# Causal mask of the diagonal score block: VectorE addition in PSUM instead of two bf16 products of TensorE per unit

## The reference, cut to what matters

```python
scale = HEAD_DIM ** -0.5                       # HEAD_DIM = 64
sc = jnp.einsum('bqhgd,bhqkd->bhgqk', qb, kg, preferred_element_type=f32) * scale
p = masked_softmax(sc, m_sel)                  # key_pos <= query position
...
diff = tq[:, None] - kpos[None, :]
m_win = (kpos[None, :] >= 0) & (diff >= 0) & (diff < WINDOW)
p = masked_softmax(sc, m_win)
...
def masked_softmax(s, mask):
    s = jnp.where(mask, s.astype(jnp.float32), NEG)      # NEG = -1e30
    return jax.nn.softmax(s, axis=-1) * mask
```

## Time and profile before

| | |
|---|---|
| median of 3 runs | 1780.42 us (1780.27 to 1780.75) |
| the profiled execution | 1778.62 us, its span 1776.8 us, mean clock granted to TensorE 0.997 of full speed |
| TensorE busy (matmuls / weight loads) | 1730.8 us (97%) / 1406.8 us (79%) |
| VectorE busy | 940.1 us (53%) |
| ScalarE busy | 651.3 us (37%) |
| GpSimd busy | 125.3 us (7%) |
| DMA | 174.86 MB, mean 98 GB/s |

### The profile page before, as it was taken

The page is one execution under the profiler, slowest core; times in us unless marked ns, Lnnn a source line. Parts: engine busy times, 40 slices in busy tenths (PEclk is TensorE's granted clock), DMA queues, the critical chain, the costliest instruction groups (busy, mean ns, idle before and its releaser), DMA issues.

```text
span 1776.8 us, 26563 instructions
## 1 busy us (share of the span) xinstructions
PE 1730.8 (97%) x10044; PEld 1406.8 (79%) x10044; DVE 940.1 (53%) x1522; ACT 651.3 (37%) x1152; POOL 125.3 (7%) x252
## 2 busy tenths in 40 slices
PE   7989999999999999999999999999999999999998
PEld 6767777788888888888887777777888888888886
DVE  5688777554454444422357977775453544444223
ACT  4334565522242232221353355654222522223213
POOL 4710000000000000000037000000000000000000
PEclk9999999999999999999999999999999999999999
DMA  7532111122523222222263421111333222222222
GB/s 258 165 97 76 57 56 48 53 103 95 168 72 106 95 94 94 94 95 95 89 246 109 102 80 54 54 49 59 107 107 125 77 95 98 101 96 94 95 95 83
DMA packets 65917, 174.86 MB, mean 98 GB/s; under 512 B 14256, under 2 KB 26576, under 8 KB 65056
## 3 DMA queue, kind: packets, MB, share of 16 engines
q1 hardware_dynamic: 40192, 140.53, 23.6%
q10 hardware_dynamic: 21888, 13.64, 3.1%
q0 software_dynamic: 3744, 19.41, 3.1%
HBM read 162.27 MB, written 7.08 MB: 95 GB/s over the span
## 4 chain that ended last, share of the span: by engine, by line
PE 88%; DVE 6%; DVEq 2%; ACT 2%; issue 1%; DMA 0%; ACTq 0%
PE ps L523 19%; PE ps L525 18%; PE ps L524 18%; PE ps L563 6%; PE ps L561 6%; PE ps L562 6%; PE ps L840 2%; PE ps L827 2%; PE ps L813 2%; DVE ta L1363 1%; PE ps L664 1%; PE ps L552 1%; PE ps L541 1%; DVE wlo L1357 1%; PE ps L816 1%
## 5 line engine op out<-in xcount | busy, mean ns | idle before, releaser
L523 PE MATMUL ps<-xh,whi 128*128 128x512 f32 x1312 | 520.2, 396 | 5.3 <-ACT gates L1173 2.1
L525 PE MATMUL ps<-xh,wlo 128*128 128x512 f32 x1312 | 512.2, 390 | 0.0
L524 PE MATMUL ps<-xl,whi 128*128 128x512 f32 x1312 | 511.5, 390 | 0.0
L1357 DVE TENSOR_TENSOR wlo<-raw,whi 128x1024 fp32r<-128x1024 f32 x264 | 324.7, 1230 | 342.0 <-ACT whi L961 331.7
L961 ACT ACTIVATE whi<-raw 128x1024 fp32r<-128x1024 f32 x264 | 278.6, 1055 | 350.7 <-PE ps L563 234.2
L523 PEld LDWEIGHTS ps<-xh,whi 128*128 128x128 f32 x1312 | 246.9, 188 | 59.5 <-DVE wlo L1357 3.6
L525 PEld LDWEIGHTS ps<-xh,wlo 128*128 128x128 f32 x1312 | 246.6, 188 | 52.7
L524 PEld LDWEIGHTS ps<-xl,whi 128*128 128x128 f32 x1312 | 247.1, 188 | 49.0
L561 PE MATMUL ps<-whi,hh 128*128 128x512 f32 x352 | 137.5, 391 | 0.0
L563 PE MATMUL ps<-whi,hl 128*128 128x512 f32 x352 | 137.0, 389 | 0.0
L562 PE MATMUL ps<-wlo,hh 128*128 128x512 f32 x352 | 137.0, 389 | 0.0
(11 more groups left out here) (335 smaller groups left out, 2325.4 us busy)
## 6 DMA issues: line engine op xcount, KB each, us to landing
raw<-wstream SPq DMA_DIRECT2D x264, 512.0 KB, 3.2
w<-w1s POOLq DMA_DIRECT2D x4, 2048.0 KB, 12.5
sm<-smalls POOLq DMA_DIRECT2D x2, 1060.0 KB, 6.6
xt<-xin ACTq DMA_DIRECT2D x4, 512.0 KB, 6.4
scratch_u<-pa ACTq DMA_DIRECT2D x8, 256.0 KB
toep<-scratch_k ACTq DMA_DIRECT2D x4, 512.0 KB
toep_b<-scratch_k ACTq DMA_DIRECT2D x4, 512.0 KB
xt<-xin POOLq DMA_DIRECT2D x4, 512.0 KB, 4.0
```

Of the source, the lines that this page charges most:

```text
L523: pe.matmul(ps[:, bank, :], wh, hi[:, k, :], start=first and i == 0, stop=False)
L524: pe.matmul(ps[:, bank, :], wh, lo[:, k, :], start=False, stop=False)
L525: m = pe.matmul(ps[:, bank, :], wl, hi[:, k, :], start=False, stop=last and i == len(blocks) - 1)
L1357: dve.tensor_tensor(wlo[:, c % 2, :], raw[:, c % 2, :], whi[:, c % 2, :].bitcast(f32), SUB).then_inc(lo_ready, 1)
```

## The change

The two bf16 products leave `scores`; the last product of query high by key low part ends the accumulation and raises `s_psum`. The bf16 copies of the identity and of the mask, their two conversions at the start, and the semaphore for them go. In `max_part`, behind the same wait for `s_psum`, VectorE adds the float32 mask `dmask` (in SBUF) to the two diagonal blocks in PSUM, in place, with one `tensor_tensor` over 128 x 2 x 128 elements, drains, and then runs the same reduction.

```diff
@@ -146,8 +146,6 @@
-    identb = own("identb", [P, P], mybir.dt.bfloat16)
-    dmaskb = own("dmaskb", [P, P], mybir.dt.bfloat16)
@@ -272,7 +270,6 @@
-        masks_ready = sem("masks_ready")
@@ -810,10 +807,8 @@
                     for a, b in ((qhi, krh), (qlo, krh), (qhi, krl)):
                         for kv in range(2):
                             rows = slice(64 * kv, 64 * kv + 64)
-                            pe.matmul(ps[:, sbank(i) + kv, 0:n], a[rows, P * t:P * t + P], b[rows, br, 0:n],
-                                      start=a is qhi and b is krh, stop=False)
-                    for kv in range(2):
-                        m = pe.matmul(ps[:, sbank(i) + kv, P * t:n], identb[:, :], dmaskb[:, :], start=False, stop=True)
+                            m = pe.matmul(ps[:, sbank(i) + kv, 0:n], a[rows, P * t:P * t + P], b[rows, br, 0:n],
+                                          start=a is qhi and b is krh, stop=b is krl)
                     m.then_inc(s_psum, 1)
@@ -863,7 +858,6 @@
-                pe.wait_ge(masks_ready, 2)
@@ -1514,8 +1508,6 @@
-                dve.tensor_copy(identb[:, :], cnv("ident")).then_inc(masks_ready, 1)
-                dve.tensor_copy(dmaskb[:, :], cnv("dmask")).then_inc(masks_ready, 1)
@@ -1792,6 +1784,9 @@
                 def max_part(i):
                     n = P * (i % 8 // 2 + 1)
                     dve.wait_ge(s_psum, l * 32 + (i + 1))
+                    diagonal = ps[:, sbank(i):sbank(i) + 2, n - P:n]
+                    tt(diagonal, diagonal, bc(cnv("dmask"), 1, 2), ADD)
+                    dve.drain()
                     dve.tensor_reduce(tiny[:, 28 + 8 * (i % 3):30 + 8 * (i % 3)], ps[:, sbank(i):sbank(i) + 2, 0:n], AX.X, MAX,
                                       negate=True).then_inc(s_max, 1)
```

## The result

The changed kernel took 1786.8 us (median of 11 runs, 1781.76 to 1790.48), the kernel before, on the same chip, 1780.42 us (median of 11, 1778.92 to 1783.43). The ratio is 1.0032, with a 95% interval of 1.0022 to 1.0042: slower, by more than 0.2% in the estimate and in the whole interval, and above the range on record (1777.8 to 1785.0). The profiled execution of the changed kernel took 1789.0 us, with a span of 1787.2 us and a mean clock of 0.989, where the one of before had 1778.62, 1776.8 and 0.997. By the timelines 4.3 of the 10.4 us lie outside the entries and the attention stages.

What follows compares the result with a forecast made beforehand. TensorE, busy for 97% of the span, was taken to bound the kernel. Two layers at +0.30 us (+0.60) plus 0.31 in the second gave +0.91 on 1780.42: 1781.3 us, range 1777.8 to 1785.0.

Steps and rivals of the forecast that it cites:

- E: TensorE's wait at the attention entry, before each layer's first transposes; forecast to grow from 0.89 to some 2 us.
- T: TensorE's wait at the half slab of turn 26 in each layer, 1.18 us before; forecast 0.75 us longer.
- What goes from TensorE: 128 mask products, two per unit; each unit gives back s = 0.075 us, bounds 0 and 0.29.
- the tile switch: Rival: switching from 64-row to 128-row products swallows the saving, s = 0; 1784.0 us, chance 0.08.
- the whole pair: Rival: the mask pair's whole record comes back on TensorE, s = 0.29; 1773.6 us, chance 0.07.
- What VectorE gets: One 128x256 PSUM addition plus drain per unit, delaying the row maximum by a = 0.53 us; bounds 0.42 and 0.80.
- Place 1: Attention entry: two additions lie in the VectorE chain the first transposes wait for; +1.06 us per layer.
- Place 2: Turns 4-6, 12-14, 20-22: two additions exceed 1.04 us slack; TensorE waits 0.24 us; +0.06 per layer, 9 savings lost.
- The late instruction in the second layer: At turn 5 a late instruction starts the VectorE chain, taking 0.31 us more slack; +0.31 us.
- Place 3: Turn 26's half-slab wait: its own addition costs +0.53 us per layer, and savings of units 26 to 28 are lost.
- The sum: Whole kernel: +0.30 us per layer, +0.60 for two, plus 0.31 in the second layer; +0.91 us, median 1781.3.
- The one on VectorE's pace: Rival: dearer PSUM writes and exponential chains becoming open waits; with a = 0.80, 1786.2 us, chance 0.08.

Runs made afterwards that it cites:

- changed, second timing: The changed kernel, unaltered, timed again in a later series: 1784.81 us, ratio 1.0027 to the kernel before.
- entry on TensorE: Changed kernel with the masks of units 0 and 1 of each layer back on TensorE: 1780.66 us, ratio 0.9998 to the kernel before.
- turn 26 on TensorE: Changed kernel with the masks of units 26 and 27 alone back on TensorE: 1781.57 us, ratio 1.0007 to the kernel before.
- both: Changed kernel with the masks of units 0, 1, 26 and 27 back on TensorE: 1777.23 us, ratio 0.998 to the kernel before.
- both, again: Changed kernel with units 0, 1, 26 and 27 masked by TensorE, timed once more: 1777.5 us, ratio 0.9985 to the kernel before.
- both waits filled: Changed kernel plus unread TensorE products, 8 ahead of the first transposes and 7 ahead of turn 26's half slab: 1783.12 us, ratio 1.0017.
- turn 26 filled: Changed kernel plus 7 unread TensorE products in the wait of turn 26 only: 1785.62 us, ratio 1.0032 to the kernel before.
- entry addition on before: Kernel before, all masks on TensorE, plus VectorE's mask addition in PSUM for units 0 and 1: 1782.91 us, ratio 1.0014.
- the same, filled: Kernel before plus VectorE's additions for units 0 and 1 and 7 unread TensorE products ahead of the first transposes: 1783.47 us, ratio 1.0017.
- the same, in SBUF: Kernel before plus two extra VectorE additions per layer for units 0 and 1, on a spare SBUF buffer: 1782.72 us, ratio 1.0016.
- no mask: Changed kernel without the addition and its drain, scores not masked at all: 1777.89 us, ratio 0.9985 to the kernel before.

## Why the prediction was wrong

**The account of all runs.** Waits and savings are read from the timelines, turn by turn and at the entry, without the half-clock turns; the clock term is the difference of the mean clocks over all runs, times 1783 us. Each against the kernel before of the same series, means in us; waits and savings are good to some 0.1:

| kernel | waits and savings | clock | sum | measured |
|---|---|---|---|---|
| changed, second timing | 0.0 | +4.3 | +4.3 | +4.8 |
| entry on TensorE | -2.0 | +1.5 | -0.5 | -0.1 |
| turn 26 on TensorE | -1.2 | +2.6 | +1.4 | +1.6 |
| both | -3.1 | -1.1 | -4.2 | -3.6 |
| both, again | -3.1 | -0.1 | -3.2 | -2.7 |
| both waits filled | 0.0 | +1.1 | +1.1 | +2.4 |
| turn 26 filled | +0.1 | +6.0 | +6.1 | +5.3 |
| entry addition on before | +2.0 | -2.1 | -0.1 | +2.6 |
| the same, filled | +2.0 | +0.9 | +2.9 | +3.1 |
| the same, in SBUF | +2.0 | 0.0 | +2.0 | +2.9 |
| no mask | -4.4 | -0.8 | -5.2 | -2.6 |

The clock term is uncertain by 0.4 to 1.4 us for each kernel (the standard error of the mean of its runs), and nine of the eleven rows agree within 1.3. The two that don't are off by 2.6 and 2.7. The changed kernel in its first timing: mean clock 0.9917, mean time 1786.3; against before's 0.995 of the later series this is 5.9 us of clock for 5.6 us more. The profiles give the same size by another way: 8 half-clock stretches behind the long waits in three executions of the changed kernel, at 1.5 us each, are 4.0 us an execution.

**The four versions of E and T.** With T and E long (mean of both timings) 1785.6; with E short 1780.5; with T short 1781.8; with both short 1777.2. Restoring E gives 5.1 us, of which 2.0 are the wait itself; restoring T gives 3.8, of which 1.2 are the wait and its three lost savings; both give 8.4, of which 3.1. What is left over is 3.1, 2.6 and 5.3, each with a standard error of 0.6 to 0.8: some 1.5 and 1.3 us at each E and T of the two layers, the size that the turns show for a half-clock stretch. This is what the forecast lacks; the two medians lie 5.5 and 3.5 us above it.

Point by point, by the prediction's own steps:

- *What goes from TensorE*, s = 0.075 a unit: 0.074 on average over the 18 turns of a layer whose savings the sum keeps (0.08 to 0.09 in most, 0.05 in turn 0, 0.04 at u = 3). The slab's load stands 0.20 us behind the 64-row pair, so nothing of the tile switch took the saving, and the whole pair (0.29) did not come back. Right.
- *What VectorE gets*, a = 0.53: operation 0.426, maximum 0.50 after the addition's start. Right within 0.03; the dear write to PSUM is excluded by the rows and by the addition into SBUF. (Where the prediction holds 0.34 us behind an undrained addition against the Trainium skill, "VectorE: DVE Perf Modes", section "The DRAIN you can't avoid", it overlooks that the section also says that a next operation that is not held starts earlier. The 0.34 us speak for a cost of the explicit drain, but not against the section.)
- *Place 1, the entry*, +1.06: +1.01 in both layers. Right.
- *Place 2, turns 6, 14 and 22*, a loss of 0.02 each: turn 6 grew by 0.06 and 0.05 us, turns 14 and 22 by up to 0.10, and the two turns ahead of each shrank by 0.17 together. So small waits are there, but they are about 0.1 us where 0.24 were forecast, and each place gains 0.07 to 0.12. The slack was a little larger than read, and the term was too high by 0.3 to 0.4 us a layer.
- *The late instruction in the second layer*, +0.31: not there; turn 6 of the second layer took 5.59, of the first 5.60. It belonged to that execution, and I read it as belonging to the kernel. Wrong by 0.3.
- *Place 3, turn 26*, +0.53 with three savings lost: turns 24 to 26 together, without half clock, grew by 0.42 in the first layer and 0.74 in the second (turn 26 alone from 6.6 to 7.2 and 7.5). Right on average.
- *The sum*, +0.91: waits and savings make about 0.0, so the forecast's own terms were 0.9 us too high together. What failed is the step from there to the time, in "The sum" and in "Where the addition lies on the path": the two waits that got longer were entered at their own length, as if TensorE came out of a wait as it went in. Behind 0.89 and 1.03 us it did; behind 2.5 and 1.8 to 2.2 us it comes out at half clock in part of the executions, for 1.4 to 1.5 us each time. None of the rivals had this, and s and a stayed inside their bounds. The one on VectorE's pace named the right side (1786.2) by the wrong mechanism: no exponential chain became the bound, and the additions were not dear.

**What stays open.** Why filling a wait brings back less than shortening it. In the profiles the half clock behind the filled wait is gone each time, and the medians fall by 1.7 to 3.7 us with both filled, and not at all with E or T filled alone, where 1.5 to 2 us were to be had at the chances seen (the differences have a standard error of 0.8 to 0.9). The mean clock (0.9944, 0.9950, 0.9920) says that half clock occurs elsewhere instead, but a profile shows one execution of 11, and which stretches trade places was not found. Also open are the two rows of the table that don't close, and whether the change alters how often half clock falls outside the stage: leaving out the one at the end, the four profiles with all masks on TensorE have 1 to 3 such stretches there, the ten others 1 to 6, too few to tell. So it is shown that the long waits cost more than their length, by restoring either; and that half clock follows them and costs what is missing, by the turns. That it is only the idling of TensorE that calls it up was not shown, and the fills speak against so simple a form.

## What to carry to other kernels

Work taken from the engine that bounds the kernel pays only in pieces that the helper hides: here 0.08 us a unit in most turns, against 0.5 us wherever the helper's chain ends a wait. Choose unit by unit: with the masks of four of the 32 units left on TensorE the same change turned from 0.3% slower to 0.15 to 0.2% faster than before. And when a change makes TensorE wait longer, do not enter the wait at its length: look at the granted clock behind it, in several executions, and shorten the wait sooner than fill it.

## What the runs showed of the hardware that was not expected

- A wait of TensorE of 0.9 to 1.5 us in this stage was never followed by half clock in the profiled executions (before, the versions with E or T short, and the one without a mask, whose E was 1.5 us); waits of 1.8 to 2.5 us were, in 13 of 22 cases where they stood unfilled. Whether one is followed by it varies between executions of one program, and between E and T of one execution. The length of the wait alone does not decide it: outside the stage waits of 1.24 us (near 521 us with T alone filled, near 1402 us with both filled) were followed by half clock too.
- The time of a program at a fixed instruction stream spreads by several us, nearly in the order of the mean clock: 1781.25 us at 0.995 to 1788.94 at 0.989 for the second timing of the changed kernel.
- A VectorE operation on 128x256 float32 from PSUM into PSUM lasts as long as into SBUF (0.426 and 0.42 us), and a drained successor starts 0.50 us after it; an undrained one started 0.34 us after an addition into SBUF.
